# Two small models fused on one core: order of the first loads, of MoBA's output product, of two latent sums and of the dilated rotations

## The reference

```python
def first_block(x, ...):                      # 2 layers
    for l in range(DEPTH):
        h = rmsnorm(x, norm1_g[l])
        x = x + gated_parallel_mixer(h, ...)  # neighbourhood, latent (MLA) and grouped-query attention, gated
        h = rmsnorm(x, norm2_g[l])
        x = x + conv_ffn(h, w_up[l], conv_w[l], conv_b[l], w_down[l])
    return rmsnorm(x, final_g)

def second_block(x, ...):                     # layer 0, then layer 1
    for layer in range(DEPTH):
        if layer % 2 == 0:
            h = _rwkv_moba_mixer(x, ...)      # RWKV-7 scan beside MoBA attention, one output product
        else:
            h = _dilated_mixer(x, ...)        # 8 heads x 3 groups of queries, masks with dilation 1, 4 and 16
        x = _layer_norm(DEEPNORM_ALPHA * x + h, ln1_g[layer], ln1_b[layer])
        x = _layer_norm(DEEPNORM_ALPHA * x + _sq_relu_mlp(x, ...), ln2_g[layer], ln2_b[layer])
    return x

# latent attention: the 384 and 256 latent features are RMS-normalised before their up-products
# RWKV-7, per head of 64: S = S*w + (S a) b^T + v k^T ;  y = S r
# dilated and MoBA heads: the first 32 of 128 features of each query and key are rotated by position
```

## Time and profile before

| | |
|---|---|
| median of three runs | 1672.24 us |
| profiled execution, its own time | 1678.14 us |
| its span (first to last instruction) | 1676.3 us |
| PE busy | 1601.7 us (96%) |
| VectorE, ScalarE, GpSimd busy | 1110.0, 917.4, 304.1 us |
| mean granted clock of TensorE | 0.987 of full speed |

### The profile page before, as it was taken

One profiled execution on the slowest core, in us unless ns is written; L12 is line 12 of the kernel. 1 busy time (PEld: TensorE's weight loads), 2 busy tenths in 40 slices (PEclk: granted clock), 3 DMA queues, 4 the chain that ended last, 5 costly groups with the idle time before them and its releaser, 6 DMA issues. The chain is left out here.

```text
span 1676.3 us, 29458 instructions
## 1 busy us (share of the span) xinstructions
PE 1601.7 (96%) x12252; PEld 1449.2 (86%) x12252; DVE 1110.0 (66%) x1746; ACT 917.4 (55%) x1471; POOL 304.1 (18%) x222
## 2 busy tenths in 40 slices
PE   6899999999998999999999998889999999899998
PEld 5889998999888899989998986768888889878886
DVE  4475656888455656568864687569944776789844
ACT  4556855766347468557654664336633566546531
POOL 0000110243000001103420253015500200007400
PEclk9899999999999999999999999999999999999999
DMA  5724445555654434545555632115565534245651
GB/s 204 199 92 152 142 153 196 178 199 182 201 167 153 138 124 148 190 172 179 201 189 188 228 115 77 54 63 190 201 226 186 192 126 151 101 170 182 242 187 74
DMA packets 45252, 272.95 MB, mean 163 GB/s; under 512 B 4672, under 2 KB 8896, under 8 KB 16064
## 3 DMA queue, kind: packets, MB, share of 16 engines
q1 hardware_dynamic: 44400, 266.36, 46.4%
q10 hardware_dynamic: 720, 4.72, 0.8%
HBM read 270.01 MB, written 1.05 MB: 162 GB/s over the span
## 5 line engine op out<-in xcount | busy, mean ns | idle before, releaser
L315 DVE TENSOR_TENSOR b_wlo<-b_wraw,b_whi 128x2048 fp32r<-128x2048 f32 (+1 forms) x264 | 573.5, 2176 | 204.7 <-PE b_ps L437 130.1
L307 ACT ACTIVATE b_whi<-b_wraw 128x2048 fp32r<-128x2048 f32 (+1 forms) x264 | 469.4, 1780 | 222.4 <-PE b_ps L437 154.1
L358 PE MATMUL b_ps<-b_H,b_whi 128*128 128x256 f32 x1784 | 508.4, 285 | 1.1 <-DVE b_wlo L315 1.1
L360 PE MATMUL b_ps<-b_H,b_whi 128*128 128x256 f32 x1784 | 500.3, 280 | 0.0
L361 PE MATMUL b_ps<-b_H,b_wlo 128*128 128x256 f32 x1784 | 500.1, 280 | 0.0
L358 PEld LDWEIGHTS b_ps<-b_H,b_whi 128*128 128x128 f32 x1784 | 337.6, 189 | 7.1 <-issue 6.4
L360 PEld LDWEIGHTS b_ps<-b_H,b_whi 128*128 128x128 f32 x1784 | 337.7, 189 | 0.7
L361 PEld LDWEIGHTS b_ps<-b_H,b_wlo 128*128 128x128 f32 x1784 | 337.5, 189 | 0.0
L404 PE MATMUL b_ps<-b_H,b_whi 128*128 128x512 f32 x448 | 155.7, 390 | 0.0
L1534 POOL TENSOR_TENSOR b_fl<-b_ab,b_fh 128x256 fp32r<-128x256 f32 x44 | 93.7, 2129 | 213.7 <-ACT b_fh L1507 213.7
L405 PE MATMUL b_ps<-b_H,b_wlo 128*128 128x256 f32 x448 | 126.3, 282 | 0.0
(11 more groups left out here) (358 smaller groups left out, 2716.9 us busy)
## 6 DMA issues: line engine op xcount, KB each, us to landing
b_wraw<-in_w SPq DMA_DIRECT2D x223, 1024.0 KB, 4.9
b_wraw<-in_w SPq DMA_DIRECT2D x37, 512.0 KB, 3.6
b_bias<-in_rpb SPq DMA_DIRECT2D x8, 512.0 KB, 11.0
b_gains<-in_gains ACTq DMA_DIRECT2D x4, 1024.0 KB, 5.0
b_wraw<-in_w SPq DMA_DIRECT2D x2, 768.0 KB, 4.3
b_cA<-in_cA SPq DMA_DIRECT2D x2, 576.0 KB, 8.3
b_X<-in_x SPq DMA_DIRECT2D x2, 512.0 KB, 4.8
out<-b_X SPq DMA_DIRECT2D x4, 256.0 KB, 2.5
```

The source lines that it names most:

```text
L307: e.activation(whi[u % NHI][:, 0:n], raw[u % NRAW][:, 0:n], ACT.Copy).then_inc(up("w_hi", "whi", u))
L315: e.tensor_tensor(wlo[u % NLO][:, 0:n], raw[u % NRAW][:, 0:n], hi.bitcast(F32), ALU.subtract).then_inc(up("w_lo", "wlo", u))
L358: e.matmul(out, wh, x.hi[:, kk, :], start=k == 0, stop=False)
L360: e.matmul(out, wh, x.lo[:, kk, :], start=False, stop=False)
```

## The change

It has six parts.

1. **Start.** The eight columns of `par` that the first gain needs are loaded by themselves, ahead of `X`; the second half of `X` comes after the first unit, the rest of `par` after the second. PE no longer waits for `par`; it does 16 transposes of the identity into a spare bank. Both engines that split weights do unit 0 in the middle of the first block's work, and unit 1 after the second block's sums. The second block is turned on PE before unit 1 is used, not after it.
2. **Latent sums.** The sum of tile 0 no longer stands between tiles 1 and 2 on PE: all three stand behind tile 2.
3. **RWKV levels.** Pieces 0 to 3 of MoBA's output product stand in front of the levels; the others and `ends` and `query` move along in `BESIDE`. The split and the first addition that belong to them stand in front of the levels on VectorE too. The first mask is made per token block.
4. GpSimd's products for `ends` wait until VectorE has made all masked matrices (`NA`).
5. **Dilated steps.** The first half of `v` stands between the last tile of heads 0 to 3 and its rotation; the last tile of heads 4 to 7 comes after `headturn` 4 and `values` 3, and its rotation after a piece of the output product (`wo` 0), with `headturn` 5, `values` 4 and `wo` 1 between the rotation and the last scores.
6. **GpSimd.** The four operations on `X` stand behind the additions of heads 0 to 3, one behind each.

```diff
     def first_rows_pe(e, w, job, key, kind):
...
-            if n == 2:
+            if n == (1 if key == "n10" else 2):
                 turn_x_pe(e, w, key, kind, 1)
...
-    def h_act(e, w, key, tb):
+    def h_act(e, w, key, tb, first=False):
         for q in range(4):
+            if first and q == 2:
+                ahead_to(e, w, split_hi, 0)
...
-    def h_dve(e, w, key, gkey, bkey, tb):
+    def h_dve(e, w, key, gkey, bkey, tb, first=False):
         for n in range(5):
+            if first and n == 3:
+                ahead_to(e, w, split_lo, 0)
...
                     tile_pe(e, w, self.lat, j)
-                    if j in (1, 2):
-                        stat_pe(e, w, self.cq[:, j - 1, :], j - 1, 3, False)
                     if j == 2:
-                        stat_pe(e, w, self.cq[:, 2, :], 2, 3, False)
+                        for k in range(3):
+                            stat_pe(e, w, self.cq[:, k, :], k, 3, False)
...
-        BESIDE = {1: ([("ob", 0)], [("ob", 1), ("ends", 0), ("ends", 1)]), 2: ([("ob", 2)], [("ob", 3), ("ends", 2), ("ends", 3)]),
-                  3: ([("ob", 4)], [("ob", 5), ("query", 0)]), 4: ([("ob", 6)], [("ob", 7), ("query", 1)]), 5: ([("ob", 8)], [("ob", 9)])}
+        BESIDE = {1: ([("ob", 4)], [("ob", 5)]), 2: ([("ob", 6)], [("ends", 0), ("ends", 1)]), 3: ([("ob", 7)], [("ends", 2), ("ends", 3)]),
+                  4: ([("ob", 8)], [("query", 0)]), 5: ([("ob", 9)], [("query", 1)])}
...
+            for n in range(4):
+                self.ob_pe(e, w, n)
             w.wait_ge(*at("cW"))
...
+            self.ob_act(e, w, 0)
...
+            self.ob_dve(e, w, 0)
+            self.ob_dve(e, w, 3)
             for n in range(1, 6):
...
                 w.wait_ge(*at("FC"))
+                w.wait_ge(*at("NA", 1, 1))
...
-            fill = [("qk", (0, j)) for j in range(16)] + [("qend", (0,)), ("v", (0,)), ("v", (1,))]
-            fill += [("qk", (1, j)) for j in range(16)] + [("qend", (1,))]
-            due = [7, 11, 15, 20, 26, 30, 34, 36]
+            fill = [("qk", (0, j)) for j in range(16)] + [("v", (0,)), ("qend", (0,)), ("v", (1,))]
+            fill += [("qk", (1, j)) for j in range(16)]
+            due = [7, 11, 15, 20, 26, 30, 34, 35]
...
             for i in range(11):
+                if i == 7:
+                    self.steps += [("wo", (0,)), ("qend", (1,)), ("headturn", (5,)), ("values", (4,)), ("wo", (1,)), ("scores", (7,))]
+                    wo = 2
+                    continue
...
         def pool(self, e, w):
-            for tb in range(2):
-                w.wait_ge(*at("full", (self.qk[0].key, 2 + tb)))
-                for plus in range(2):
-                    gains_pool(e, w, "l20", 2, tb, plus)
             for what, i in self.steps:
                 if what == "scores":
-                    scores_pool(e, w, self.att, *i)
+                    n, = i
+                    scores_pool(e, w, self.att, n)
+                    if n < 4:
+                        gains_pool(e, w, "l20", 2, n // 2, n % 2)
...
     def tensor_program(e):
         w = Waits(e)
         w.wait_ge(*at("c1"))
-        w.wait_ge(*at("par"))
         banks.assign(lin=ALL, att=ALL)
+        for i in range(WARM):
+            e.transpose(banks.tiles[STAT][:, 0:P], ident, ident)
...
     def sync_program(e):
         w = Waits(e)
         e.dma_start(c1[:, :], dram["c1"]).then_inc(up("ld_c", "c1", by=16), 16)
-        for tb in range(2):
-            e.dma_start(X[:, tb, :], dram["x"][:, tb, :]).then_inc(up(f"ld_x{tb}", "x", tb, by=16), 16)
-        e.dma_start(par[:, :], dram["par"]).then_inc(up("ld_p", "par", by=16), 16)
+        e.dma_start(par[:, 0:8], dram["par"][:, 0:8]).then_inc(up("ld_p0", "par0", by=16), 16)
+        x_load(e, 0)
+        loads[1] = [lambda e, w: x_load(e, 1)]
+        loads[2] = [lambda e, w: e.dma_start(par[:, 8:], dram["par"][:, 8:]).then_inc(up("ld_p", "par", by=16), 16)]
```

More of the change, by code:

```diff
@@ L269, in program @@
     scr = [scrs[:, i * T:i * T + T] for i in range(NSCR)]
-    STAT = 7
+    STAT, WARM = 7, 16
     ALL, SOME, ATT = list(range(7)), [0, 1, 2], [3, 4, 5, 6]
@@ L2331, in scan_dve @@
             flat = lambda t: t.rearrange("p b f i -> p (b f) i")
-            for par in range(2):
-                w.wait_ge(*at("full", ("tn", par)))
-                e.tensor_tensor(flat(XX[:, par]), banks.tile(("tn", par))[:, :].rearrange("p (g i) -> p g i", g=8), wide("lev0", 8), ALU.mult).then_inc(banks.free(("tn", par)))
-            for par in range(2):
-                w.wait_ge(*at("free", ("tn", par)))
-                e.tensor_tensor(flat(XX[:, par]), flat(XX[:, par]), wide("id64", 8), ALU.add).then_inc(up("inv", "XX", 0, 0, par))
-                sig.same(("XX", 0, 1, par), ("XX", 0, 0, par))
-            for tbk in range(2):
+            for tbk in range(2):
+                for par in range(2):
+                    w.wait_ge(*at("full", ("tn", par)))
+                    ins = e.tensor_tensor(XX[:, par, tbk, :, :], banks.tile(("tn", par))[:, T * tbk:T * tbk + T].rearrange("p (g i) -> p g i", g=4), wide("lev0", 4), ALU.mult)
+                    if tbk:
+                        ins.then_inc(banks.free(("tn", par)))
+                        sig.same(("lev0", 1, par), ("free", ("tn", par)))
+                    else:
+                        ins.then_inc(up("lev0", "lev0", 0, par))
+                for par in range(2):
+                    w.wait_ge(*at("lev0", tbk, par))
+                    e.tensor_tensor(XX[:, par, tbk, :, :], XX[:, par, tbk, :, :], wide("id64", 4), ALU.add).then_inc(up("inv", "XX", 0, tbk, par))
                 for par in range(2):
@@ L2581, in scalar_program @@
         for tb in range(2):
+            for j in range(2):
+                rms_sum_act(e, w, "n10", j, tb, ("x", tb))
             if tb:
                 ahead_to(e, w, split_hi, 1)
-            for j in range(2):
-                rms_sum_act(e, w, "n10", j, tb, ("x", tb))
-            h_act(e, w, "n10", tb)
+            h_act(e, w, "n10", tb, first=tb == 0)
         for l in range(2):
@@ L2597, in vector_program @@
         w.wait_ge(*at("c1"))
-        w.wait_ge(*at("par"))
+        w.wait_ge(*at("par0"))
         for tb in range(2):
+            rms_diag_dve(e, w, "n10", tb)
             if tb:
                 ahead_to(e, w, split_lo, 1)
-            rms_diag_dve(e, w, "n10", tb)
-            h_dve(e, w, "n10", "norm1_g0", None, tb)
+            h_dve(e, w, "n10", "norm1_g0", None, tb, first=tb == 0)
+        w.wait_ge(*at("par"))
         for l in range(2):
@@ L2622, in pool_program, with x_load @@
         mlps[1].pool(e, w)
+    def x_load(e, tb):
+        e.dma_start(X[:, tb, :], dram["x"][:, tb, :]).then_inc(up(f"ld_x{tb}", "x", tb, by=16), 16)
     def sync_program(e):
```

## The result

The changed kernel took 1663.31 us (median of 8 runs, 1657.64 to 1669.12), the kernel before 1672.11 us beside it (8 runs, 1667.41 to 1679.06). The ratio is 0.9948, with a 95% interval of 0.9923 to 0.9973. The forecast was 1663.4 us, a ratio of 0.9947. The profiled execution took 1669.02 us, its span 1666.6 us against 1676.3.

What follows compares the result with a forecast made beforehand. PE bounds the kernel, busy 1601.7 of 1676.3 us, so gains come from its idle and half-clock time. 2.8 + 3.2 + 1.3 + 0.8 + 0.7 = 8.8 us gives 1663.4 us; range 1659 to 1667, 8 in 10 for 1655 to 1671.

Steps and rivals of the forecast that it cites:

- Start: Up to the first tile: PE begins 1.5 us earlier and low parts come sooner; 2.8 us won, range 1.5 to 3.6.
- Latent sums: Two layers: tile 2 fills the wait before the sums; 1.6 us each, 3.2 us won, range 1.2 to 8.0.
- the price of the old wait: Latent sums: a 3.47 us wait, after which tile 2's products take 5.3 us at half clock, 2.7 at full.
- Levels: RWKV levels: output-product matmuls fill PE's 2.19 us mask wait; 1.3 us won, from 0.5 lost to 3.2 won.
- PE waits until 1048.2, 1.2 us: Level 1: with the split and addition ahead of the masks, a mask of about 0.6 us makes PE wait 1.2 us.
- Dilated heads 0 to 3: GpSimd's operations each hold VectorE 2.45 us, two old stalls go; 0.8 us won, from 3 lost to 7.5 won.
- Tail: End of the dilated heads: scores 7 come 3.0 us later, `headturn` 7 slightly earlier; 0.7 us won, 1.0 lost to 1.5 won.
- A: Rival: GpSimd does not hold VectorE on the path; dilated heads win 7.5 instead of 0.8, 1656.7 us; chance 0.17.
- B: Rival: the waits only change their place, in all stages; 4.3 us won, 1667.9 us; chance 0.23.
- C: Rival: GpSimd's four operations in the dilated heads take 4.46 us each, not 2.45; 14.8 lost, 1678.2 us; chance 0.10.
- D: Rival: the start's change does nothing, the remaining loads set the pace; 1666.2 us; within the forecast range's chance of 0.50.

Runs made afterwards that it cites:

- u_lat: The changed kernel with part 2 (latent sums) undone and all else kept: 1663.63 us, 0.9955 of the kernel before.
- again: The changed kernel run once more, unchanged: 1664.31 us, 0.9954 of the kernel before.
- f_pool: The changed kernel with GpSimd's four operations moved ahead of the additions, to where VectorE waits for the exponentials: 1661.83 us, 0.994 of the kernel before.
- u_pool: The changed kernel with part 6 undone, GpSimd's four operations in front of the heads again: 1662.54 us, 0.9941 of the kernel before.
- u_start: The changed kernel with part 1 (start) undone and parts 2 to 6 kept: 1667.53 us, 0.9978 of the kernel before.

## Why the forecast was right, and where it was not

**Start, 2.8 us forecast.** Measured 3.5 (34.2 to 34.5 without, 30.1 to 31.4 with it). The mechanism held; the term was a little small, since the second low part came at 21.5 (forecast 22.0) and no wait for the third was left.

**Latent sums, 3.2 us forecast.** The first two profiles seem to bear it out: 47.77 - 46.34 and 22.97 - 20.10 make 4.3 us. The runs do not: without part 2 the stretches are as short as with it. The step that failed is the price of the old wait, which I took from one execution as fixed (5.6 and 3.47 us) with its half-speed stretch behind it. The waits are 1.97 and 1.35 us in u_lat; in layer 1 this goes with the landing of a weight unit, which moves by some 4 us between executions, and the clock behind a stall with chance. That an earlier start makes this wait short is not shown: the latest squares of all stand in a kernel with part 1. That ScalarE's split makes a new wait was right (0.97 to 1.91 us, most often 1.91, with part 2; under 0.6 where the split stands behind). Where the unit lands late, part 2 does fill a wait (3.8 us in the changed kernel, 6.0 before); what that is worth on average is too small for these runs.

**Levels, 1.3 us forecast (range from 0.5 lost to 3.2 won).** Measured nothing, or up to 0.5 lost (81.9 against 81.4). The step "PE waits until 1048.2, 1.2 us" was mis-sized: 2.10, since the masks wait for the split and the addition together. And the sum missed that PE's instruction packets pace the levels, so that the gaps called "issue" grow where other waits go: 2.65 to 4.90 us.

**Dilated heads 0 to 3, 0.8 us forecast.** VectorE is stopped for an operation's whole length, as forecast, and PE waits before scores 1 and 2; the waits were 1.26 and 2.27 instead of 2.6 and 2.9 us, since VectorE did have slack: a hold of 2.2 us in head 0 made a wait of 1.26, so 0.9 us of it. From the stage's start to scores 3 the changed kernel took 89.6 us and again 90.6, before 92.4: 1.8 to 2.8 won.

**Tail, 0.7 us forecast.** Scores 7 waited 2.90 us (forecast about 4) at full clock, and from scores 6 to the end of the stage it took 38.85 and 38.09 us instead of 39.27: 0.4 to 1.2 (the mean of the twelve executions with part 5 is 38.8, so 0.5). `headturn` 7 came 8.3 us behind scores 7 (forecast 8.0 to 9.3). Together the dilated mixer won 3.2 us where 1.5 was forecast (means 178.15 and 181.36). Of this the clock may be nearly all: the one execution of the kernel before lost an estimated 6.8 us to half speed in this stretch, the seven others 2.9 on average, which leaves 174.6 before and 175.2 after. Whether the shorter waits or chance took the half-speed stretches away stays open.

**Sum.** By the stretches it is 3.5 + 0 - 0.5 + 3.2 = 6.2 us, with up to 1.3 more if the latent means (44.3 and 20.2 with part 2, 44.5 and 21.3 without) are taken at their word. The medians give 8.8, with 4.5 to 12.9 in the interval, which holds both. Two terms were too small by 0.7 and 1.7 us, two too large by 2 to 3 and 1.3 to 1.8. That the total came out at 1663.3 is luck in part: these errors cancel. The undoing runs are surer than the stretches, since they rest on medians: 3 to 4 us for part 1, 1.5 to 2.5 for part 5, nothing that shows for part 2, for parts 3 and 4 and for part 6. What of the remaining 1.3 to 2.6 us is real stays open.

**Rivals.** A (GpSimd doesn't hold VectorE) fell for the changed kernel, but its price came true once the operations stood elsewhere: up to scores 3 f_pool wins 7.4 us over the kernel before (84.95 us for 92.38), where A had 7.5 with 2.9 of it clock; here an estimated 3.4 is clock. B (waits only move) is what happened to the latent sums and the levels. C fell: the operations took 2.40 to 2.42 us. The 4.46 us of the earlier trace rows was GpSimd held by VectorE's split, the same exclusion seen from the other side; in u_pool it is 4.30 and 4.34. D (the start does nothing) fell with u_start.

## What to carry to other kernels

GpSimd's long elementwise work belongs where VectorE waits for another engine, started by the event that begins that wait: it cost nothing there, and 2.2 us each where it began 3 us later. A wait read from one execution is not a price: ask what makes it long (here, when a load lands), how far that moves between executions, and how much of a stretch is its clock. Where a stall is removed from a dense run of small matmuls, look for the gaps called "issue", for the instruction queue's packets in the DMA view, and for the load that now starts earlier.

## What the runs showed of the hardware

- GpSimd and VectorE exclude each other for whole instructions when VectorE's has its inputs in SBUF: 0.56 us became 2.74 beside an operation of 2.41, and 1.62 beside one of 1.29. GpSimd is held in the same way: 2.4 became 4.3 to 4.5 beside a split of 2.3.
- A VectorE instruction that reads PSUM (L856) was not held: 0.42 us beside GpSimd.
- The same wait of 2.27 us was followed by a granted clock of 1.00 in one execution and 0.53 in another. The fourteen executions had 20 to 44 us at half speed, and two of the same kernel 30.7 and 44.3.
- In runs of 64x64 matmuls PE stops for 0.5 to 2.0 us at matmuls that stand about 126, or a multiple of that, apart; 56 of the 57 gaps over 0.5 us end 1.2 to 1.6 us behind the end of a packet of the instruction queue q8. While a load of 1 MB moved 393 GB/s, no such packet started, and the gap was 4.61 us.
